# Block 1 of a two-matrix-split gated trunk moved to seven products, with its weight sums formed while block 0 reads the raw weights

## The reference

```python
h = rmsnorm(x, g_pre[l])
proj = h @ w_in[l]                                   # 1024 x 10240
(a_u, a_v, a_z, b_a, b_b, b_z, c_x, c_z, d_b, d_c, d_x, d_z, gate_logits) = jnp.split(proj, SPLITS, axis=-1)
out_a = gmlp_spatial(a_u, layernorm(a_v, ...), w_s[l], b_s[l]) * jax.nn.silu(a_z)
out_b = jax.nn.silu(layernorm(causal_depthwise(glu, conv_b_w[l]) + bias, ...)) * jax.nn.silu(b_z)
out_c = multiscale_pool(ext_c, start_pos, pool_w[l], pool_scale[l]) * jax.nn.silu(c_z)
out_d = d_b * causal_depthwise(ext_d, conv_d_w[l]) * jax.nn.silu(d_z)
gates = jax.nn.sigmoid(gate_logits + b_gate[l])      # four gates of width 1024
merged = sum(gates[i] * (out_i @ w_branch[l, i]) for i in range(4))
x = x + rmsnorm(merged @ w_out[l], g_post[l])
```

## Time and profile before

| | us |
|---|---|
| median of 3 runs | 2377.5 (2376.88 to 2377.93) |
| the profiled execution | 2379.08 |
| its span in the trace | 2377.0 |
| PE busy in it | 2356.2 |
| DVE / ACT / POOL busy | 1568.0 / 442.9 / 633.1 |

### The profile page before, as it was taken

The page is one execution under the profiler, slowest core; times in us unless marked ns, Lnnn a source line. Parts: engine busy times, 40 slices in busy tenths (PEclk is TensorE's granted clock), DMA queues, the critical chain, the costliest instruction groups (busy, mean ns, idle before and its releaser), DMA issues.

```text
span 2377.0 us, 34997 instructions
## 1 busy us (share of the span) xinstructions
PE 2356.2 (99%) x13240; PEld 2086.9 (88%) x13240; DVE 1568.0 (66%) x2347; ACT 442.9 (19%) x646; POOL 633.1 (27%) x423
## 2 busy tenths in 40 slices
PE   9999999999999999999999999999999999999998
PEld 7888888888788888788888899999898999999998
DVE  7886887855666577775266866776337776577643
ACT  5223222323112111122101100111110110010111
POOL 4435545455545646656200000000100000000000
PEclk9999999999999999999999999999999999999999
DMA  8977878788998998999765599999875458988884
GB/s 329 321 249 278 308 261 326 271 296 329 376 326 288 364 328 321 371 325 363 292 252 186 204 322 374 306 331 323 271 252 163 157 186 287 332 281 267 282 284 173
DMA packets 286115, 686.63 MB, mean 289 GB/s; under 512 B 19665, under 2 KB 97873, under 8 KB 258577
## 3 DMA queue, kind: packets, MB, share of 16 engines
q1 hardware_dynamic: 273520, 652.18, 78.3%
q10 hardware_dynamic: 12448, 32.49, 3.6%
HBM read 514.14 MB, written 170.46 MB: 288 GB/s over the span
## 4 chain that ended last, share of the span: by engine, by line
PE 88%; DVE 5%; issue 2%; POOL 1%; POOLq 1%; DMA 1%; DVEq 1%; ACT 1%; SPq 0%; ACTq 0%
PE acc L1928 47%; PE acc L2146 18%; PE side L2157 7%; PE side L2072 4%; PE side L2146 4%; PE acc L2306 3%; PE side L2306 3%; POOL s_lo L669 1%; DMA w_pair<-split_main 1%; PE acc L2303 1%; PE side L2303 1%; PE side L2100 1%; PE side L2090 1%; DVE t_sum L1413 0%; PE acc L2336 0%
## 5 line engine op out<-in xcount | busy, mean ns | idle before, releaser
L1928 PE MATMUL acc<-h_hi,w_pair 128*128 128x512 f32 x2752 | 866.2, 390 | 6.4 <-DMA w_pair<-split_main 6.2
L1928 PEld LDWEIGHTS acc<-h_hi,w_pair 128*128 128x128 f32 x2752 | 517.4, 188 | 116.2 <-issue 7.7
L1928 PE MATMUL acc<-h_lo,w_pair 128*128 128x512 f32 x1376 | 536.1, 390 | 0.0
L1200 DVE SCALAR_TENSOR_TENSOR cb<-glu,col,cb 128x512 f32<-128x512 f32 x600 | 425.0, 773 | 18.9 <-issue 10.9
L648 POOL TENSOR_TENSOR w_pair<-w_raw,w_pair 128x1024 fp32r<-128x1024 f32 x118 | 268.4, 2286 | 273.1 <-ACT w_pair L779 258.1
L678 POOL TENSOR_TENSOR rstd<-msq,nhalf 128x5 f32<-128x5 f32 (+4 forms) x19 | 19.9, 1047 | 1126.7 <-DVE msq L1110 532.3
L1928 PEld LDWEIGHTS acc<-h_lo,w_pair 128*128 128x128 f32 x1376 | 258.6, 188 | 53.4
L2146 PE MATMUL acc<-t_hi,chunk 128*128 128x256 f32 (+1 forms) x1344 | 266.8, 287 | 1.3 <-DVE merged L1505 1.3
L2146 PEld LDWEIGHTS acc<-t_hi,chunk 128*128 128x128 f32 x1344 | 216.6, 189 | 2.0 <-DVE merged L1505 1.7
L2146 PE MATMUL acc<-h_hi,chunk 128*128 128x256 f32 (+1 forms) x1008 | 205.1, 289 | 2.6 <-issue 1.5
L2146 PE MATMUL acc<-t_lo,chunk 128*128 128x256 f32 (+1 forms) x672 | 193.0, 287 | 0.0
(11 more groups left out here) (327 smaller groups left out, 3405.6 us busy)
## 6 DMA issues: line engine op xcount, KB each, us to landing
w_pair<-split_main SPq DMA_DIRECT2D x118, 1024.0 KB, 7.2
chunk<-split_main SPq DMA_DIRECT2D x226, 512.0 KB, 5.8
chunk<-s_parts SPq DMA_DIRECT2D x200, 512.0 KB, 6.2
split_main<-w_pair SPq DMA_DIRECT2D x88, 1024.0 KB, 6.7
w_raw<-in_w_main SPq DMA_DIRECT2D x88, 512.0 KB, 5.1
chunk<-split_branch SPq DMA_DIRECT2D x62, 512.0 KB, 4.5
s_raw<-in_w_main SPq DMA_DIRECT2D x100, 256.0 KB, 6.0
s_parts<-s_hi SPq DMA_DIRECT2D x50, 512.0 KB, 5.2
```

The lines of the kernel that those rows point to most:

```text
L1200: dve.scalar_tensor_tensor(dst, src, c1("conv_w", c * CK + t), dst, ALU.mult, ALU.add)
L1928: ins = pe.matmul(acc[:, s, b, 0:m], w_k[:, wt, wk], mv_[:, k, t0:t0 + m], start=(k == 0 and n == 0), stop=(k == nk - 1 and n == 2))
```

## The change

Block 1 becomes a seven-product block like 2 and 3 (`SEVEN0 = 1`). Block 1 therefore needs the weights' sums, and they are made in block 0 out of the raw tiles while these lie in `w_raw`: when POOL comes to the low part of the second tile of a pair, it first waits for the store of the previous pair's sums, forms the four sums into the one buffer `s_sum`, and then takes the low part. SP reloads the first tile's buffer only when the sums are formed, stores the right half alone of a second tile, and stores the sums raw (`s_parts`, 1 MB a pair). The four sum chunks are loaded raw (256 KB each) into half a chunk buffer; ACT casts each (`chunk_cast`) and POOL takes its low part (`chunk_low`) in blocks 1 to 3, and PE waits for `c_lo_done` in place of the landing. The low parts of the activations' sums move from DVE to POOL, and the fourth sum is formed ahead of the two first gates' merges. Loops of SP and POOL in block 0 are written out.

```diff
-SEVEN0 = 2
+SEVEN0 = 1
+SUM_AT = (1, 2, 3, 5)
+PAIR_UNITS = []
+for _n, _q in PAIRS:
+    if _n[0] == "G":
+        _f = UNIT0["G2b"] if (_n, _q) == ("G2", 3) else UNIT0[_n] + 4 * (_q + (_n == "G0"))
+        PAIR_UNITS.append((_f, _f + 2))
+    else:
+        PAIR_UNITS.append((UNIT0[_n] + 2 * _q, UNIT0[_n] + 2 * _q + 1))
...
     @blk.sync
-        def raw_load(u, r, src, n):
+        def raw_load(u, src, n):
-            if not isinstance(u, int) or u >= RING:
+            if u >= RING:
                 sp.wait_ge(w_lo_done, u - RING + 1)
+                if u - RING in PAIR_OF:
+                    sp.wait_ge(s_summed, SUM_RANK[PAIR_OF[u - RING]] + 1)
...
+        def split_store(u):
...
+            sp.wait_ge(w_lo_done, u + 1)
...
+            elif second:
+                dst, src = split_main[unit_pieces(name, r)[0][1], :, :, WB:DM], f(w_pair[u % RING])[:, :, WB:DM]
...
+            sp.dma_start(dst, src).then_inc(split_stored[u % RING], 16)
+            if second:
+                sp.wait_ge(s_summed, SUM_RANK[p] + 1)
+                sp.dma_start(s_parts[p, :, :, :], s_sum[:, :, :]).then_inc(s_stored, 16)
...
+            dst = chunk_raw[n % CHUNKS][:, :] if STREAM[n][0] == "sum" else f(chunk[n % CHUNKS])
...
     @blk.gpsimd
+        def lo(u, n):
             pool.wait_ge(w_hi_done, u + 1)
+            s, p = u % RING, PAIR_OF.get(u)
+            if p is not None and u == PAIR_UNITS[p][1]:
+                pair_weights(p)
             pool.tensor_tensor(w_lo[s][:, 0:n], w_raw[s][:, 0:n], f(w_hi[s])[:, 0:n],
                                ALU.subtract).then_inc(w_lo_done, 1)
+        def pair_weights(p):
...
+            if SUM_RANK[p]:
+                pool.wait_ge(s_stored, 16 * SUM_RANK[p])
+            pool.tensor_tensor(s3, a21, a11, ALU.subtract)
             pool.drain()
+            pool.tensor_tensor(s1, a22, a21, ALU.add)
+            pool.tensor_tensor(s2, a22, s3, ALU.add)
             pool.drain()
+            pool.tensor_tensor(s4, a12, s2, ALU.subtract)
             pool.drain().then_inc(s_summed, 1)
...
+        def chunk_low(j, p, at):
+            n = PAIR_AT[j, p][0] + at
+            pool.wait_ge(c_hi_done, sum_no(j, p, at) + 1)
+            pool.tensor_tensor(chunk[n % CHUNKS][:, 1, :], chunk_raw[n % CHUNKS][:, :], f(chunk[n % CHUNKS])[:, 0, :],
+                               ALU.subtract).then_inc(c_lo_done, 1)
...
+            for t, casts in ((1, 2), (3, 3), (2, 4)):
+                t_low(j, t, casts)
+            for at in SUM_AT[:3]:
+                chunk_low(j, 0, at)
+            t_low(j, 4, 4)
...
     @blk.scalar
-        def s_cast(j, u):
+        def chunk_cast(j, p, at):
+            n = PAIR_AT[j, p][0] + at
+            act.wait_ge(chunk_landed[n % CHUNKS], 16 * (n // CHUNKS) + 16)
+            act.activation(chunk[n % CHUNKS][:, 0, :], chunk_raw[n % CHUNKS][:, :], ACT.Copy).then_inc(c_hi_done, 1)
...
                 copy_p1(j, p)
+                chunk_cast(j, p, SUM_AT[3])
+                if p + 1 < NPAIR:
+                    chunk_cast(j, p + 1, SUM_AT[0])
+                    chunk_cast(j, p + 1, SUM_AT[1])
...
     @blk.vector
-                t_sums((3, 0), (3, 1), (3, 2))
-                def fourth_and_lows():
-                    t_sums((4, 0), (4, 1))
-                    for t in (2, 3, 1, 4):
-                        t_low(t)
-                merge(0, 0, 1, after={0: fourth_and_lows})
+                t_sums((3, 0), (3, 1), (3, 2), (4, 0), (4, 1))
+                merge(0, 0, 1)
...
     @blk.tensor
+                    product(n + 1, tt[2], bank[1], sum_no(j, p, 1))
```

More of the change, by code:

```diff
@@ L206, in build @@
     chunk = [sb(f"chunk{c}", [P, 2, WB], F32R, addr=pair_at + c * 2 * WB * 4) for c in range(CHUNKS)]
-    s_parts = nc.dram_tensor("s_parts", (NPAIR, P, 2, 4 * WB), F32).ap()
+    chunk_raw = [sb(f"chunk_raw{c}", [P, WB], addr=pair_at + (c * 2 + 1) * WB * 4) for c in range(CHUNKS)]
+    s_parts = nc.dram_tensor("s_parts", (NPAIR, P, 4, WB), F32).ap()
     split_main = nc.dram_tensor("split_main", (MAIN, P, 2, DM), F32).ap()
@@ L572, in s_store @@
-        def s_store(h):
-            q, hx, b = h // 2, h % 2, h % 3
-            sp.wait_ge(s_lo_done, h + 1)
-            for n, part in enumerate((s_hi[b], s_lo[b])):
-                dst = s_parts[q, :, n, :].rearrange("p (c n) -> p c n", c=8)
-                sp.dma_start(dst[:, hx::2, :], f(part)).then_inc(s_stored[b], 16)
+            for r in range(count):
+                u = UNIT0[name] + r
+                if u:
+                    m = unit_pieces(name, r)[0][1]
+                    if name[0] == "G" and r % 2:
+                        raw_load(u, raw_branch_rows(m), WB)
+                    else:
+                        raw_load(u, raw_rows(m), DM)
+                if u >= RING:
+                    split_store(u - RING)
+                if u == RING - 1:
+                    for dst, src in [(bs_bc[:, :, :], bs_rows.partition_broadcast(P)),
+                                     (ws[:, :, :], ws_t), (tmp[:, 0:P], mask_t), (poolw[:, :, :], pool_w),
+                                     (smp_g[:, :, :], st_conv), (smp_c[:, :, :], st_pool), (smp_d[:, :, :], st_short)]:
+                        sp.dma_start(dst, src).then_inc(const_loaded, 16)
@@ L580, in chunk_source @@
+        for u in range(UPB - RING, UPB):
+            split_store(u)
+        for r in range(RING):
+            sp.wait_ge(split_stored[r], 16 * (UPB // RING))
         def chunk_source(kind, m, c):
@@ L584, in chunk_source @@
             if kind == "sum":
[L585 removed]
+                return s_parts[m, :, c, :]
             return split_branch[m, :, :, :]
@@ L724, in _ @@
                     power(TPB + 1)
[L725 to L726 removed]
+                if name == "O":
+                    h_part(1, r)
         for j in range(1, NBLK):
             last = j == NBLK - 1
[L729 to L750 removed]
+            power(TPB + 1)
@@ new lines, in _ @@
+            power(TPB)
+            if last:
+                power(1, DEC)
+            for t, casts in ((1, 2), (3, 3), (2, 4)):
[3 more added lines that the diff above has]
+            t_low(j, 4, 4)
+            for p, pair in enumerate(PAIRS):
+                chunk_low(j, p, SUM_AT[3])
+                if pair == ("G2", 2) or pair == ("G3", 0) and not last:
+                    power(TPB + 1)
+                if p + 1 < NPAIR:
+                    for at in SUM_AT[:3]:
+                        chunk_low(j, p + 1, at)
@@ L857, in load_x_rows @@
             if j == NBLK - 2:
-                for h in range(2):
-                    act.dma_start(x_dec[h][0:DEC, :], x_rows[SEQ:SEQ + DEC, h * WB:(h + 1) * WB]).then_inc(dec_loaded, 16)
+                for n in range(4):
+                    act.dma_start(x_dec[n][0:DEC, :], x_rows[SEQ:SEQ + DEC, n * HW:(n + 1) * HW]).then_inc(dec_loaded, 16)
         def load_xres(j):
@@ L1447, in _ @@
                     if j == SEVEN0 and c == 0:
-                        for b in range(3):
-                            dve.wait_ge(s_stored[b], 32 * ((NH + 2 - b) // 3))
+                        dve.wait_ge(s_stored, 16 * NPAIR)
                     conv_step(j, 12 + c)
```

239 lines of the change are left out of this document (63 added, 176 removed).

## The result

The changed kernel takes 2535.4 us in the median of four runs (2531.6 to 2539.8), the kernel before 2377.4; the ratio is 1.066 [1.065, 1.068]. That is 158 us slower, where 61 us were forecast, and 45 us above the range. The profiled execution took 2535.3 us with a span of 2533.5.

What follows compares the result with a forecast made beforehand. PE, busy 99% of the span, was taken to bound the kernel. 2377.5 - 26.1 (block 1) + 85 (block 0's sums) + 2 (other edits) = 2438 us, range 2392 to 2490.

Steps and rivals of the forecast that it cites:

- mechanism of block 0: Block 0: making the sums there stretches D and G pairs past PE's periods, +85 us (40 to 141).
- D loop: Block 0, D and Z pairs: waiting on the one sums buffer takes 17.0 us against PE's 10.9, +61 us (47 to 85).
- G loop: Block 0, G pairs: sums, reload, store landing, cast and low parts take 18.4 us against PE's 16.3, +30 us (2 to 56).
- Three loops: Block 0: loops said to close over the sums, each to be added up and compared with PE's period.
- 30 - 6: Block 0: 30 us lost over 14 G pairs, less 6 us (0 to 9) that the three-unit ring hides once.
- ring loop: Block 0, G pairs: the tile buffer's reload and split-part store, cast, low parts and sums, 18.4 us (16.4 to 20.3).
- Block 1's gain: Block 1, fifth G0 unit to O: seven products bring 363.3 us to block 2's 337.3, -26.1 us.
- The other edits: Blocks 1 to 3: moved low parts, moved fourth sum, chunk casts and low parts together cost +2 us (-3 to +12).
- hidden, but thinly: Pairs of blocks 1 to 3: POOL's chunk low parts fit DVE's slack, 0 to +10 us, 0.5 taken.
- the path over the casts ahead of the second sigmoid: Pair stretch's start: ACT casts the fourth sum and two chunks first, some 2.3 us; entry edits -1 to +2 a block.
- Blocks 1 to 3 slow down as well: Rival, G1 and G2 of blocks 1 to 3: DVE lacks slack, each pair costs PE 1 to 2 us, +38; 8 in 100.
- PE's clock: Rival, D and Z of block 0: half clock makes pairs 21.8 us, 48 us on top, 2486 us; 7 in 100.

Runs made afterwards that it cites:

- Run 2: Changed kernel with sums formed for every pair but only the first pair's stored, and all pairs loading those; 2475.6 us.
- run 8: Changed kernel with only the first pair's sums formed, sum chunks loaded ready, activations' low parts and fourth sum placed as before the change; 2356.2 us.
- run 5: Changed kernel without the sum chunks' casts and low parts: each sum chunk loaded as 512 KB with two ready parts; 2498.2 us.
- run 4: Changed kernel with the fourth sum of activations formed behind the first gate's merge again, low parts still on POOL; 2527.3 us.
- run 3: Changed kernel without POOL's four sum operations for all pairs but the first, every store, wait and load kept; 2409.0 us.
- run 9: Changed kernel with block 0's split-part stores issued ahead of reloads and the sums stored right behind the first tile's reload; 2473.9 us.
- run 1: Changed kernel with SP storing the sums as soon as formed, ahead of the first tile's reload and split-part stores; 2498.8 us.

## Why the prediction missed

- **Direction and mechanism of block 0: right.** The sums of a pair take 6.1 us in the mean (forecast 6.3 in D, 5.9 in G), D pairs are 18.1 us apart (eight of them 145.1 us by their first sums at 250.62 and 395.67), PE waits on POOL's `w_pair`, POOL on `s_parts`. D and Z lost 58 + 14 = 72 us for a forecast 61.
- **D loop: a chosen size was off.** The sum of means was 17.9 and I took 17.0 "since a stage that is stretched by half has DVE and POOL meeting less often". The discount had no ground: the sums stayed near their mean, and the second tile's low part was at 2.7 us. Within the loop, the landing was 7.6, not 6.7, and the half store's issue 1.14, not 1.65. (The high end adds up to 19.2, not 19.4; nothing hangs on it.)
- **G loop: the step that failed in block 0.** "Three loops close over these sums", says the prediction, and it adds up two. The third is the sums' store in G, behind the issues of a whole burst: 20.5 us. G pairs lost the other 55 us where 30 - 6 were forecast. Run 2 takes this loop away, and G1 stays at 20.4 and G3 at 18.8: the ring loop that I did price, at 18.4, was itself 0.4 to 2 us short. In the pair from 410.82 to 430.60, 19.8 us, the four sums take 7.0 us (to 417.84), not 5.9, and the two low parts behind the cast 4.5, not 3.9; the landing, 6.6, was right. Priced rightly it alone gives 14 x 2.5 = 35 to 14 x 4.1 = 57 us.
- **Block 1's gain: the number was right and was given away.** -26.1 us from the comparison of two stretches of before; run 8 has 467.7 us against 495.2, -27.5. The change as made has -2.4.
- **The other edits, +2 (-3 to +12): the worst step.** They cost 57.7 us: some 40 for the chunks (run 5) and 14 to 19 for the entries (run 8), with the slower clock behind the waits in both. For the chunks I had read DVE's 4.0 us free a pair in G1 against 2.5 us of meetings, and called it "hidden, but thinly". A mean slack over a section isn't the slack of the operation that PE waits for: DVE's `zc` comes right behind four convolution operations, which took 3.60 us in one such place and 2.74 in the earlier trace rows. For the entries I priced the removed low parts and the new casts, but not the merge behind the moved sum; a list of what stands behind the moved sum on DVE would have found it. And the path over the casts ahead of the second sigmoid, which I had named and given next to nothing, makes PE wait 4.5 us a block once the merge is out of its way (run 4).
- **Rivals.** "Blocks 1 to 3 slow down as well" had +38 and a chance of 8 in 100, and stood as an alternative to the forecast. It is all but independent of block 0 (run 3), so both happened; 2438 + 38 = 2476 was its number, with each cost at its low side. The range was built from cases that exclude each other, and so had no room for a sum of two. PE's clock didn't stay at half: the granted clock was 0.85 over 253 to 400 us in D, so about 44 us of these 147 at 0.50 if the rest was at 1.00, and the period there was that of the loop, which PE isn't in. Where the clock did cost time is blocks 1 to 3, some 13 us, and there the prediction hadn't looked for it.
- **Turns and landings.** The convolution takes 929 ns with GpSimd's low parts beside it and 747 without. That agrees with the Trainium skill (GPSIMD Engine Reference, Key points), by which the two engines share their SBUF interfaces. The sums' store landed after 8.1 us in the median, after 6.6 in run 9, where it went out second in its burst, and after 4.9 in run 1, where it went out first. By the Trainium skill's figures (DMA: Bandwidth & Descriptors, Anatomy of one DMA) I estimate 4.4 us for it; the page fits them to transfers that GpSimd issues, and these are SP's. Only run 1 comes near that. That the rest is what stood ahead in the queue fits the order of the three, but no run takes it apart.

## What to carry to other kernels

For each resource with one buffer, close its loop in every section that uses it, with all issues that stand ahead in the queue, since the loop changes with the section. When work moves to an engine that takes turns with the one on which PE's gates depend, compare with the slack of the operation that PE waits for, not with a section's mean. And risks in different places of a kernel add: a range needs their sums, not the worst of them.
